# Low parts of the weights by an accumulating transfer in place of a subtraction on GpSimd

## The chip, the cores and the metric

The kernel runs on one core of one Trainium2 chip. The metric is the device time of one execution in microseconds; the whole input, weights included, lies in HBM at the start.

## What is computed

Two stacks of two layers each run over one sequence of 512 tokens of width 1024, in fp32. The first stack (`first_block`) has a convolution-and-attention mixer in layer 0, a gated linear recurrence in layer 1, and after each a squared-ReLU MLP of width 4096:

```python
for layer in range(DEPTH):
    h = rmsnorm(x, mix_norm[layer])
    y = mixer_ab(h, ...) if layer % 2 == 0 else mixer_c(h, ...)
    x = x + y
    x = x + sq_relu_mlp(rmsnorm(x, mlp_norm[layer]), w_up[layer], w_down[layer])
return rmsnorm(x, final_norm)
```

The second stack puts 16 meta tokens ahead (528 rows) and has, twice, a mixer of a gated delta rule and an indexed sparse attention, and a gated MLP of width 2816 with a short convolution:

```python
h = jnp.concatenate([meta, x], axis=1)
for l in range(DEPTH):
    n = rms_norm(h, norm_mix[l])
    h = h + hybrid_mixer(n, w_in[l], ...)
    n = rms_norm(h, norm_ffn[l])
    h = h + conv_gated_mlp(n, w_up[l], conv_ffn[l], w_down[l])
return h[:, N_META:]
```

## The kernel before, in words

Every product with a weight matrix is made with split operands. A value v is written as a high part (v rounded to fp32r, which TensorE reads in one pass) and a low part, v minus the high part, also fp32r. A product is three matmuls into the same PSUM bank: high weight by high value, high weight by low value, low weight by high value. In the code these are `for i, (w, v) in enumerate(((wh, hi), (wh, lo), (wl, hi)))`.

The weights come as 436 pieces of up to 512 KB (128 partitions x 1024 fp32). SyncE loads them in the order of use into `w_raw`, a ring of four slots (`load_piece`, L698). ScalarE copies a piece into `w_hi` (L1535), GpSimd subtracts, `w_lo` = `w_raw` - `w_hi`, in steps of 256 columns (L772). `w_hi` and `w_lo` are rings of eight half slots. The class `Order` plans what goes where. It holds 878 operations: a `whole` piece takes two half slots, the others one.

- In the mixers and at the start of each feed a piece is used whole (192 pieces).
- In the four feeds (mlp0, mlp1, and the gated MLPs layer0, layer1) the weights into the hidden layer are taken in pairs of pieces, and a pair is multiplied by seven half products in place of eight (a Strassen-like scheme): a11, s1, a12, s2, s4, s3, a22. Four of them need sums of weights that VectorE makes: s1, s2 and s4 into `weight_sum` (L2697, L2699, L2701), s3 in place in the raw slot of the pair's second piece (L2703). Between s3 and a22, and after a22, stand halves (`down`) of pieces of the second matrix. mlp0 and mlp1 have 14 pairs each with 4 such halves per pair (11 operations, 4 loads); layer0 and layer1 have 19 pairs each with 2 (9 operations, 3 loads).

The engines run in program order and wait on semaphores. What sets the order around the change:

- ScalarE (`split_one`) waits until the piece has landed, or the sum is made, and until the product that used the half slot before is done (`w_used`), then writes the high part and counts up `w_hi`. Between its splits it does the other work of the stage. In a feed it copies three products of each pair out of PSUM (`keep_product`, L1821, tile `kept_product`), which TensorE waits for before s2, s4 and s3 (L1035). Before each such copy it makes every split that is allowed by then (`split_before`).
- GpSimd does nothing but the low parts, in the same order, and counts up one semaphore `w_lo` per operation.
- TensorE waits for `w_lo` of an operation before its matmuls (L1035 for the half products, L1090 and L1094 for the down products, L800 for whole pieces).
- SyncE loads piece p + 4 when the last low part that reads the slot of piece p is made (`order.freed`). With three pieces to a gated pair, the second piece of the next pair needs the slot of this pair's first piece, which is free after the low part of s3.
- VectorE makes s1 of the next pair only when both its pieces have landed, and overwrites a `weight_sum` only when its old low part is made.
- In a gated feed VectorE takes a22 out of PSUM (L3181), multiplies (L3185, L3130) and makes s3 of the next pair (L2703).

```python
pool.wait_ge(w_hi, o + 1)
for a in range(0, n, 2 * P):
    z = min(a + 2 * P, n)
    i = pool.tensor_tensor(wl[:, slot, at + a:at + z], source[:, a:z],
                           wh[:, slot, at + a:at + z].bitcast(F32), ALU.subtract)
i.then_inc(w_lo, 1)
```

Of the kernel before, what the change touches and what calls it, by code (L numbers as in the profile page):

```python
# [220 lines left out]
class Order:  # L221
# [169 lines left out]
def build(nc, stream, xt, vec1, vec2, const1, const2, dist, lru_w, meta, saved_x, out):  # L391
# [172 lines left out]
    w_hi, w_lo, w_used = sem("w_hi_ready"), sem("w_lo_ready"), sem("w_product_done")  # L564
# [10 lines left out]
    mean_full, cent_ready, var_full, ln_root = sem("mean_full"), sem("centred_then_lru_rate"), sem("variance_full"), sem("ln_root_then_lru_rate_exp")  # L575
    ln_sq = sem("ln_square")
    ln_scaled, y_hi, y_ready = sem("ln_scaled"), sem("y_hi_ready"), sem("y_ready")
    bias_ready = sem("alibi_ready")
    vt_full, vt_copied, spread_copied = sem("v_turned"), sem("v_copied"), sem("head_scales_copied")
    s_full, s_shift, s_exp, heads_scaled = sem("scores_full"), sem("scores_shifted"), sem("scores_exp"), sem("head_scales_and_heads_ready")  # L580
    pt_full, pt_ready, o_full = sem("probs_turned"), sem("probs_t_ready"), sem("attn_out_full")
    xc_ready, ri_full, ri_sig, tanh_ready = sem("lru_conv_ready"), sem("head_scales_then_lru_gates_full"), sem("lru_sigmoid"), sem("lru_tanh")
    gelu_ready = sem("gelu_ready")
    xc_gated, x_final = sem("lru_input_gated"), sem("x_final")
    a_ready, m_ready, mult_ready, yc_ready = sem("lru_decay"), sem("lru_square"), sem("lru_mult"), sem("lru_out")
# [6 lines left out]
    vtok_full, vtok_ready = sem("v_tokens_full"), sem("v_tokens_ready")  # L592
# [4 lines left out]
    g_in, gcol_full = sem("decay_logs"), sem("decay_sums")  # L597
    norms_turned, first_tap = sem("norms_turned"), sem("first_tap_ready")
# [12 lines left out]
    ux_full, ux_ready, uy_full, uy_ready = sem("join_full"), sem("join_ready"), sem("last_join_full"), sem("last_join_ready")  # L611
    uw_full, uw_ready = sem("w_full"), sem("w_ready")
    uv_full, uv_ready, uso_full, us_ready, uo_done = sem("v_new_full"), sem("v_new_ready"), sem("step_full"), sem("state_ready"), sem("step_out_taken")
    oz_ready, o_hi, o_ready = sem("out_gated"), sem("out_hi_ready"), sem("out_lo_ready")
# [4 lines left out]
    meta_gained, both_sums, x_root = sem("meta_gained"), sem("both_sums_ready"), sem("x_root_ready")  # L619
    gate_sent = sem("gate_sent")  # L620
    gate_back = [sem(f"gate_back_{n}") for n in range(4)]

# [70 lines left out]
    def _(sp):  # L693
# [54 lines left out]
        for p in range(RAW_SLOTS, pieces):  # L748
            sp.wait_ge(w_lo, order.freed(p - RAW_SLOTS))
# [25 lines left out]

    @block.tensor
    def _(pe):
# [3 lines left out]
        def product(job, hi, lo, cols, wait=None):  # L781

            p = at["piece"]
            pe.wait_ge(w_lo, used(p + 1))
# [40 lines left out]
        def fill_wide(blocks):  # L825

            for _ in range(blocks):
                p, b = at["piece"], at["block"]
                if b == 0:
                    pe.wait_ge(w_lo, used(p + 1))  # L830
# [9 lines left out]
        def out_blocks(p, a, z, order, hi, lo):  # L840

            if a == 0:
                pe.wait_ge(w_lo, used(p + 1))
# [11 lines left out]
        def first_product():  # L855
# [3 lines left out]
            for b in range(KT + 4):  # L859
# [4 lines left out]
                if b == 4:  # L864
                    pe.wait_ge(w_lo, 1)
# [6 lines left out]
        def mixer0():  # L872
# [10 lines left out]
            def turn_v(pair):  # L883
# [7 lines left out]
                mm.then_inc(vt_full, 1)  # L891

            def scores(n):
# [3 lines left out]
                for hh in range(2):  # L897
                    half = slice(DH * hh, DH * hh + DH)
                    pe.matmul(aux[:, hh, 0:P * (i + 1)], qs[half, pair, P * i:P * i + P], ks[half, pair, 0:P * (i + 1)],
                              start=True, stop=True).then_inc(s_full, 1)  # L900
# [2682 lines left out]
```

## Time and profile before

| | |
|---|---|
| median of 3 runs | 2898.32 us (2896.45 to 2898.58) |
| the profiled execution | 2896.0 us |
| its span | 2894.2 us |
| granted TensorE clock, mean | 0.988 |
| TensorE matmul busy | 2737.9 us, 95% |
| VectorE busy | 2023.6 us, 70% |
| GpSimd busy | 1879.7 us, 65% |
| ScalarE busy | 1219.6 us, 42% |
| moved by DMA | 271.25 MB |

The span runs from the first to the last instruction of one profiled execution; the time of that execution is 1.8 us longer. Busy shares are means over stages with different limits, so the stages have to be looked at one by one. mlp0 lies at about 250 to 620 us, mlp1 at about 720 to 1090, the feed of layer0 at about 1640 to 2000, that of layer1 at about 2540 to 2890; the mixers lie between.

### The profile page before, as it was taken

What the parts mean: (1) busy time and instruction counts of PE and PEld (TensorE: products, weight loads), DVE (VectorE), ACT (ScalarE), POOL (GpSimd) and SP (SyncE); (2) the same over time, 40 slices, a digit from 0 to 9 for tenths busy, and PEclk for the clock granted to TensorE, in tenths of its full rate; (3) what the DMA queues carried; (4) which work ended last, traced back from release to release, by engine and by line L of the source; (5) the groups of instructions that cost most, each with busy time, mean ns of one, the idle gap of its engine ahead of it and who ended that gap; (6) DMA issues with size and microseconds to landing.
All of it is one profiled execution on the core that took longest, in us unless ns stands there. A gap on an engine that the chain in (4) does not pass through costs nothing.

```text
span 2894.2 us, 48195 instructions
## 1 busy us (share of the span) xinstructions
PE 2737.9 (95%) x18508; PEld 2470.3 (85%) x18508; DVE 2023.6 (70%) x3175; ACT 1219.6 (42%) x2145; POOL 1879.7 (65%) x2144
## 2 busy tenths in 40 slices
PE   9988999999899999999999889999999899988998
PEld 6767989877798988988899888999988799978887
DVE  8958666686666668897544777776797645767775
ACT  4454434455343444433343334445343353334442
POOL 6425998856599885532236589997542225489997
PEclk9999999999999999999999999999999999999999
DMA  5112332332233233323324122233322324122222
GB/s 185 59 34 75 96 110 94 111 102 75 72 100 105 95 117 111 110 66 96 105 83 133 54 81 93 91 100 108 100 78 88 89 87 142 60 86 84 88 90 93
DMA packets 122676, 271.25 MB, mean 94 GB/s; under 512 B 22864, under 2 KB 57040, under 8 KB 122192
## 3 DMA queue, kind: packets, MB, share of 16 engines
q1 hardware_dynamic: 73104, 245.98, 26.4%
q10 hardware_dynamic: 49344, 22.19, 2.8%
q8 instruction: 148, 2.42, 0.3%
q14 instruction: 80, 0.66, 0.1%
HBM read 249.52 MB, written 18.61 MB: 93 GB/s over the span
## 4 chain that ended last, share of the span: by engine, by line
PE 68%; DVE 22%; issue 5%; ACT 2%; POOL 1%; DMA 1%; ACTq 0%; SPq 0%; DVEq 0%
PE aux L1035 16%; PE acc L800 15%; PE acc L1090 13%; PE acc L1287 5%; PE acc L1094 3%; PE acc L849 3%; PE aux L1301 3%; DVE index_score L3227 2%; PE acc L1268 2%; PE aux L1268 2%; DVE best L3220 2%; DVE w_raw L2703 1%; DVE unit_b L3130 1%; POOL w_lo L772 1%; PE acc L833 1%
## 5 line engine op out<-in xcount | busy, mean ns | idle before, releaser
L772 POOL TENSOR_TENSOR w_lo<-w_raw,w_hi 128x256 fp32r<-128x256 f32 x1744 | 1478.5, 881 | 931.9 <-ACT w_hi L1535 928.1
L1535 ACT ACTIVATE w_hi<-w_raw 128x512 fp32r<-128x512 f32 (+2 forms) x680 | 487.2, 738 | 381.6 <-PE acc L800 143.7
L772 POOL TENSOR_TENSOR w_lo<-weight_sum,w_hi 128x256 fp32r<-128x256 f32 x396 | 407.2, 1054 | 61.2 <-ACT w_hi L1535 56.7
L1035 PE MATMUL aux<-token_sum_hi,w_hi 128*128 128x264 f32 (+1 forms) x1056 | 304.7, 289 | 77.6 <-ACT kept_product L1821 40.8
L800 PE MATMUL acc<-n_hi,w_hi 128*128 128x264 f32 (+1 forms) x1336 | 337.6, 317 | 8.8 <-DVE unit_a L3136 6.5
L800 PE MATMUL acc<-n_lo,w_hi 128*128 128x264 f32 (+1 forms) x1336 | 326.6, 309 | 0.0
L800 PE MATMUL acc<-n_hi,w_lo 128*128 128x264 f32 (+1 forms) x1336 | 326.0, 308 | 0.0
L1035 PE MATMUL aux<-token_sum_hi,w_lo 128*128 128x264 f32 (+1 forms) x1056 | 300.5, 285 | 0.0
L1035 PE MATMUL aux<-token_sum_lo,w_hi 128*128 128x264 f32 (+1 forms) x1056 | 300.3, 284 | 0.0
L1035 PEld LDWEIGHTS aux<-token_sum_hi,w_hi 128*128 128x128 f32 x1056 | 201.0, 190 | 90.8 <-issue 67.0
L1090 PE MATMUL acc<-hidden_hi,w_hi 128*128 128x512 f32 x688 | 271.9, 395 | 2.1 <-DVE hidden_lo L3109 2.1
L1090 PE MATMUL acc<-hidden_lo,w_hi 128*128 128x512 f32 x688 | 272.4, 396 | 0.0
L1090 PE MATMUL acc<-hidden_hi,w_lo 128*128 128x512 f32 x688 | 272.0, 395 | 0.0
L1535 ACT ACTIVATE w_hi<-weight_sum 128x512 fp32r<-128x512 f32 x198 | 124.8, 630 | 338.6 <-DVE weight_sum L2697 239.2
L2711 DVE TENSOR_TENSOR unit_a<-aux,kept_product 128x256 f32<-128x256 f32 (+1 forms) x160 | 68.3, 428 | 263.5 <-PE aux L1035 195.5
L800 PEld LDWEIGHTS acc<-n_hi,w_hi 128*128 128x128 f32 x1336 | 218.8, 189 | 37.8 <-issue 21.8
L800 PEld LDWEIGHTS acc<-n_lo,w_hi 128*128 128x128 f32 x1336 | 217.4, 189 | 14.3 <-issue 2.6
L1035 PE MATMUL aux<-n_hi,w_hi 128*128 128x264 f32 (+1 forms) x792 | 225.5, 285 | 4.2 <-POOL w_lo L772 4.0
L800 PEld LDWEIGHTS acc<-n_hi,w_lo 128*128 128x128 f32 x1336 | 217.4, 189 | 11.9
L1035 PE MATMUL aux<-n_lo,w_hi 128*128 128x264 f32 (+1 forms) x792 | 224.5, 283 | 0.0
L1035 PE MATMUL aux<-n_hi,w_lo 128*128 128x264 f32 (+1 forms) x792 | 224.5, 283 | 0.0
L2726 DVE TENSOR_TENSOR x<-x,acc 128x512 f32<-128x512 f32 (+1 forms) x224 | 153.2, 684 | 89.8 <-PE acc L1090 80.3
(525 smaller groups left out, 6364.3 us busy)
## 6 DMA issues: line engine op xcount, KB each, us to landing
w_raw<-in_stream SPq DMA_DIRECT2D x420, 512.0 KB, 3.6
unit_blocks<-unit_scratch ACTq DMA_DIRECT2D x26, 256.0 KB, 3.9
w_raw<-in_stream SPq DMA_DIRECT2D x16, 384.0 KB, 3.2
unit_scratch<-unit_staged ACTq DMA_DIRECT2D x20, 256.0 KB, 2.6
saved_x<-x SPq DMA_DIRECT2D x2, 2112.0 KB, 9.6
x<-saved_x SPq DMA_DIRECT2D x16, 264.0 KB, 2.7
saved_gates<-root ACTq DMA_DIRECT2D x12, 264.0 KB, 2.0
unit_scratch<-unit_staged ACTq DMA_DIRECT2D x1, 2560.0 KB, 15.1
```

The source lines that it names most:

```text
L772: i = pool.tensor_tensor(wl[:, slot, at + a:at + z], source[:, a:z], wh[:, slot, at + a:at + z].bitcast(F32), ALU.subtract)
L800: last = pe.matmul(o, w[:, slot_of(p), P * b:P * b + P], r, start=(b == 0 and i == 0), stop=(b == n - 1 and i == 2))
L849: mm = pe.matmul(acc[:, bank_of(p), :], w[:, slot_of(p), P * b:P * b + P], v[b], start=(n == 0 and i == 0), stop=(n == KT - 1 and i == 2))
L1035: mm = pe.matmul(aux[:, bank, 0:width], w[:, slot, at_ + P * b:at_ + P * b + P], v[:, b, :], start=(opens and b == 0 and i == 0), stop=(b ...
L1090: mm = pe.matmul(into, lhs, v[:, e % 2, b, ROW], start=(b == 0 and i == 0), stop=(b == n - 1 and i == 2))
L1094: mm = pe.matmul(banks[:, s, 0:HALF], lhs, v[:, e % 2, b, HALF * s:HALF * s + HALF], start=(b == 0 and i == 0), stop=(b == n - 1 and i == 2))
L1268: mm = pe.matmul(banks[:, 2 * g + s, 0:HALF], w[:, slot_of(p), P * b:P * b + P], v[:, b, HALF * s:HALF * s + HALF], start=(b == 4 * g and ...
L1287: mm = pe.matmul(acc[:, s, 0:HALF], w[:, slot_of(p), P * b:P * b + P], v[:, b, HALF * s:HALF * s + HALF], start=(b == 0 and i == 0), stop= ...
L1301: return pe.matmul(out, lhs, rhs, start=start, stop=stop)
L1535: act.activation(wh[:, slot, at_:at_ + n], weights_of(o), ACT.Copy).then_inc(w_hi, 1)
L2711: dve.tensor_tensor(into, aux[:, bank, 0:width], kept_product[:, kept, 0:width], ALU.add)\
L2726: dve.tensor_tensor(xm, xm, a, ALU.add).then_inc(taken, c.made(taken))
```

## The change

ScalarE now makes two activations per operation: first the negated value, rounded to fp32r, into `w_lo` (which is minus the high part), then the high part into `w_hi`. GpSimd no longer computes. For each operation it waits for the high part and issues one DMA that adds the fp32 values of `w_raw` (or `weight_sum`) onto `w_lo`, so that `w_lo` holds value minus high part when it lands. The one counter `w_lo` becomes eight semaphores, one per half slot of the ring, each raised by 16 per landing; everyone who waited for `w_lo` (TensorE, SyncE, VectorE) now waits for the landing of the operation it needs. `freed` returns the list of all operations that read a raw slot, and SyncE waits for each. To have eight semaphores free, several others with disjoint times of use are merged under one name.

```diff
@@ class Order
+        self.turn, turns = [], [0] * (2 * W_SLOTS)
...
+            turns[self.place[-1]] += 1
+            self.turn.append(turns[self.place[-1]])
...
     def freed(self, p):
 
-        found = [n + 1 for n, (kind, piece, _) in enumerate(self.ops) if piece == p or (piece == p - 1 and kind == "a22")]
-        paired = [n + 1 for n, (kind, piece, _) in enumerate(self.ops) if piece == p and kind == "s3"]
-        return paired[0] if paired else max(found)
+        return [n for n, (kind, piece, _) in enumerate(self.ops)
+                if (piece == p and kind in ("whole", "down", "a11", "a12", "s3")) or (piece == p - 1 and kind in ("a22", "s3"))]
@@ build
-    w_hi, w_lo, w_used = sem("w_hi_ready"), sem("w_lo_ready"), sem("w_product_done")
+    w_hi, w_used = sem("w_hi_ready"), sem("w_product_done")
+    w_lo = [sem(f"w_lo_landed_{n}") for n in range(2 * W_SLOTS)]
...
+    def low_landed(o):
+
+        return w_lo[order.place[o]], 16 * order.turn[o]
@@ SyncE
         for p in range(RAW_SLOTS, pieces):
-            sp.wait_ge(w_lo, order.freed(p - RAW_SLOTS))
+            for o in order.freed(p - RAW_SLOTS):
+                sp.wait_ge(*low_landed(o))
             load_piece(p)
@@ GpSimd
             pool.wait_ge(w_hi, o + 1)
-            for a in range(0, n, 2 * P):
-                z = min(a + 2 * P, n)
-                i = pool.tensor_tensor(wl[:, slot, at + a:at + z], source[:, a:z],
-                                       wh[:, slot, at + a:at + z].bitcast(F32), ALU.subtract)
-            i.then_inc(w_lo, 1)
+            pool.dma_start(wl[:, slot, at:at + n], source, accum_op=ALU.add).then_inc(low_landed(o)[0], 16)
@@ TensorE, at each wait for a low part
-                pe.wait_ge(w_lo, o + 1)
+                pe.wait_ge(*low_landed(o))
@@ ScalarE
             n = width_of(o)
+            act.activation(wl[:, slot, at_:at_ + n], weights_of(o), ACT.Copy, scale=-1.0)
             act.activation(wh[:, slot, at_:at_ + n], weights_of(o), ACT.Copy).then_inc(w_hi, 1)
@@ VectorE, weight_sum_of
-            if name != "s3" and at["split"][n]:
-                dve.wait_ge(w_lo, at["split"][n])
-            at["split"][n] = order.index[name, p, u] + 1
+            if name != "s3" and at["split"][n] is not None:
+                dve.wait_ge(*low_landed(at["split"][n]))
+            at["split"][n] = order.index[name, p, u]
```

On ScalarE, in the feed of layer0, around the first `kept_product` of a pair: the high parts of s3 and of the two down halves, the copy of a11's product, the high part of a22, and the copy of s1's product. Before:

```order
L1535 ACTIVATE w_hi<-weight_sum 128x512 x2
L1535 ACTIVATE w_hi<-w_raw 128x512 x3
L1821 ACTIVATE kept_product<-aux 128x264
L1535 ACTIVATE w_hi<-w_raw 128x512
L1821 ACTIVATE kept_product<-aux 128x264
```

The same place in the changed program:

```order
L1538 ACTIVATE w_lo<-w_raw 128x512
L1539 ACTIVATE w_hi<-w_raw 128x512
L1538 ACTIVATE w_lo<-w_raw 128x512
L1539 ACTIVATE w_hi<-w_raw 128x512
L1538 ACTIVATE w_lo<-w_raw 128x512
L1539 ACTIVATE w_hi<-w_raw 128x512
L1825 ACTIVATE kept_product<-aux 128x264
L1538 ACTIVATE w_lo<-w_raw 128x512
L1539 ACTIVATE w_hi<-w_raw 128x512
L1825 ACTIVATE kept_product<-aux 128x264
```

Six activations stand ahead of the first copy where three stood, and two ahead of the second where one stood.

On GpSimd, over one pair of the same feed (s2 and s4 from `weight_sum`; then s3, two down halves, a22 and the next a11 from `w_raw`; the next s1; the next a12). Before:

```order
L772 TENSOR_TENSOR w_lo<-weight_sum,w_hi 128x256 x4
L772 TENSOR_TENSOR w_lo<-w_raw,w_hi 128x256 x10
L772 TENSOR_TENSOR w_lo<-weight_sum,w_hi 128x256 x2
L772 TENSOR_TENSOR w_lo<-w_raw,w_hi 128x256 x2
```

Now:

```order
L777 DMA w_lo<-weight_sum 128x512 x2
L777 DMA w_lo<-w_raw 128x512 x5
L777 DMA w_lo<-weight_sum 128x512
L777 DMA w_lo<-w_raw 128x512
```

The order is the same; two subtractions of 256 columns have become one transfer of 512.

## Rows read from the trace of the kernel before

**Rows 1.** The page, part 1: busy us, share of the span and count by engine
```profile
PE 2737.9 (95%) x18508; PEld 2470.3 (85%) x18508; DVE 2023.6 (70%) x3175; ACT 1219.6 (42%) x2145; POOL 1879.7 (65%) x2144
```

**Rows 2.** Windows: stretch, its length, busy us (x count) by engine, clock, DMA share, GB/s
```profile
core 0: us, PE busy (x) PEld busy (x) DVE busy (x) ACT busy (x) POOL busy (x), PEclk, DMA share, GB/s
...
300.00:400.00 100.00, 100.00 (x620) 89.34 (x619) 64.79 (x87) 40.56 (x78) 93.98 (x108) 1.00 0.32 101
...
1200.00:1300.00 100.00, 97.28 (x781) 90.44 (x780) 95.22 (x228) 40.94 (x59) 42.50 (x53) 1.00 0.25 75
...
1800.00:1900.00 100.00, 93.83 (x763) 92.73 (x762) 73.58 (x96) 41.65 (x81) 99.14 (x105) 1.00 0.29 93
```

**Rows 3.** Waits of TensorE over the span: us in total, times, longest us
```profile
PE aux L1035 <- ACT kept_product L1821: 40.8, 33, 1.8
PE aux L1035 <- POOL w_lo L772: 24.8, 7, 8.6
PE aux L1035 <- DVE root L2711: 14.9, 12, 2.6
```

**Rows 4.** The page, part 5: GpSimd's two groups
```profile
L772 POOL TENSOR_TENSOR w_lo<-w_raw,w_hi 128x256 fp32r<-128x256 f32 x1744 | 1478.5, 881 | 931.9 <-ACT w_hi L1535 928.1
...
L772 POOL TENSOR_TENSOR w_lo<-weight_sum,w_hi 128x256 fp32r<-128x256 f32 x396 | 407.2, 1054 | 61.2 <-ACT w_hi L1535 56.7
```

**Rows 5.** Timeline of ScalarE, feed of layer0: start us, us for all, instruction, [idle before]
```profile
1785.33 1.67 ACT L1535 ACTIVATE w_hi<-w_raw 128x512 fp32r<-128x512 f32 x3 [3.26 <-DVE w_raw L2703]
1786.91 0.37 ACT L1821 ACTIVATE kept_product<-aux 128x264 f32<-128x264 f32 x1
...
1804.21 0.37 ACT L1821 ACTIVATE kept_product<-aux 128x264 f32<-128x264 f32 x1
```

**Rows 6.** Timeline of TensorE there: the first matmul of s2
```profile
1787.43 0.36 PE L1035 MATMUL aux<-token_sum_hi,w_hi 128*128 128x264 f32 x1 [1.03 <-ACT kept_product L1821]
```

**Rows 7.** Timeline of VectorE there
```profile
1780.72 0.68 DVE L2701 TENSOR_TENSOR weight_sum<-w_raw,weight_sum 128x512 f32<-128x512 f32 x1
...
1782.05 0.43 DVE L3181 TENSOR_TENSOR root<-aux,norm_scale 128x264 f32<-128x264 f32 x1
1782.40 0.59 DVE L3185 TENSOR_TENSOR root<-root,norm_scale 128x264 f32<-128x264 f32 x1
1783.12 1.03 DVE L3130 TENSOR_TENSOR unit_b<-squares,root 128x528 f32<-128x528 f32 x1
1784.08 1.22 DVE L2703 TENSOR_TENSOR w_raw<-w_raw 128x512 f32<-128x512 f32 x1
...
1791.90 1.22 DVE L2697 TENSOR_TENSOR weight_sum<-w_raw 128x512 f32<-128x512 f32 x1
...
1794.04 2.29 DVE L3122 SCALAR_TENSOR_TENSOR unit_b<-unit_a,vec,unit_b 128x528 f32<-128x528 f32 x2
```

**Rows 8.** The page, part 3: the queue of the weight loads, share of 16 engines
```profile
q1 hardware_dynamic: 73104, 245.98, 26.4%
```

**Rows 9.** DMA issues: count, KB each, us to landing; and one load's issue, feed of layer0
```profile
w_raw<-in_stream SPq DMA_DIRECT2D x9, 512.0 KB, 3.7
...
unit_blocks<-unit_scratch ACTq DMA_DIRECT2D x26, 256.0 KB, 3.9
...
unit_scratch<-unit_staged ACTq DMA_DIRECT2D x20, 256.0 KB, 2.6
...
1787.48 0.33 SPq L698 DMA_DIRECT2D w_raw<-in_stream  x1
```

**Rows 10.** DMA from 1780 to 1830 us in 40 slices: busy tenths, GB/s
```profile
DMA  0000004730369300000057105792000000670048
GB/s 0 0 0 0 0 0 36 262 134 0 26 256 419 144 0 0 0 0 0 7 85 282 66 0 52 269 419 98 0 0 13 0 0 0 88 305 26 0 69 331
```

**Rows 11.** Timeline of ScalarE in mlp0, the same copy in two pairs
```profile
397.75 0.39 ACT L1821 ACTIVATE kept_product<-aux 128x256 f32<-128x256 f32 x1
...
418.75 0.39 ACT L1821 ACTIVATE kept_product<-aux 128x256 f32<-128x256 f32 x1
```

**Rows 12.** Timeline of GpSimd, feed of layer0: s3, two down halves, a22, next a11
```profile
1786.05 8.56 POOL L772 TENSOR_TENSOR w_lo<-w_raw,w_hi 128x256 fp32r<-128x256 f32 x10
```

More of the change, by code:

```diff
@@ L783, in product @@
             p = at["piece"]
-            pe.wait_ge(w_lo, used(p + 1))
+            pe.wait_ge(*low_landed(used(p)))
             one, paired = cols == SEQ, job >= starts.get("layer0", pieces)
@@ L829, in fill_wide @@
                 if b == 0:
-                    pe.wait_ge(w_lo, used(p + 1))
+                    pe.wait_ge(*low_landed(used(p)))
                     pe.wait_ge(taken, evicted(p) - 1)
@@ L842, in out_blocks @@
             if a == 0:
-                pe.wait_ge(w_lo, used(p + 1))
+                pe.wait_ge(*low_landed(used(p)))
                 pe.wait_ge(taken, evicted(p) - (1 if shares(p) else 3))
@@ L864, in first_product @@
                 if b == 4:
-                    pe.wait_ge(w_lo, 1)
+                    pe.wait_ge(*low_landed(0))
                 if b >= 4:
@@ L890, in turn_v @@
                     mm = pe.transpose(acc[:, 1, P * a:P * a + P], vs[:, pair, P * a:P * a + P], ident)
-                mm.then_inc(vt_full, 1)
+                mm.then_inc(vtok_full, 1)
             def scores(n):
@@ L1124, in narrow_product @@
             p = at["piece"]
-            pe.wait_ge(w_lo, used(p + 1))
+            pe.wait_ge(*low_landed(used(p)))
             if half == 0:
@@ L1259, in branch @@
             if g:
-                pe.wait_ge(w_lo, used(p + 1))
+                pe.wait_ge(*low_landed(used(p)))
                 pe.wait_ge(taken, evicted(p) - (1 if m else 0))
@@ L1280, in fill @@
             if at["block"] == 0:
-                pe.wait_ge(w_lo, used(p + 1))
+                pe.wait_ge(*low_landed(used(p)))
                 pe.wait_ge(taken, evicted(p))
@@ L1617, in norm_twice @@
             act.wait_ge(ss_full, c.next(ss_full))
-            act.wait_ge(both_sums, 1)
+            act.wait_ge(both_sums, c.next(both_sums))
             act.activation(rt[:, :], ssq[:, :], ACT.Sqrt, scale=1.0 / D).then_inc(root_ready, c.made(root_ready))
@@ L1660, in copy_v @@
             def copy_v(pair):
-                act.wait_ge(vt_full, pair + 1)
+                act.wait_ge(vtok_full, c.next(vtok_full))
                 act.activation(vt[:, :, P * pair:P * pair + P], acc[:, 1, :].rearrange("p (a d) -> p a d", a=4),
@@ L1711, in mixer0 @@
                         act.wait_ge(cent_ready, c.next(cent_ready))
-                        act.activation(zpad[:, i, 0:SEQ], cv[:, i, :], ACT.Square).then_inc(ln_sq, c.made(ln_sq))
+                        act.activation(zpad[:, i, 0:SEQ], cv[:, i, :], ACT.Square).then_inc(vtok_ready, c.made(vtok_ready))
                 if n == 13:
@@ L1721, in mixer0 @@
                     for i in range(4):
-                        act.wait_ge(ln_scaled, c.next(ln_scaled))
+                        act.wait_ge(both_sums, c.next(both_sums))
                         act.activation(zpad[:, i, 0:SEQ], cv[:, i, :], ACT.Silu, scale=vec("ab_ln_g", i),
@@ L1745, in gates_of @@
                 act.activation(tb[:, h, :], rb[:, h, :], ACT.Tanh, scale=c8[:, 2, h:h + 1])\
-                    .then_inc(tanh_ready, c.made(tanh_ready))
+                    .then_inc(first_tap, c.made(first_tap))
             def decay(h):
@@ L1761, in high_of @@
             def high_of(h):
-                act.wait_ge(yc_ready, h + 1)
+                act.wait_ge(oz_ready, c.next(oz_ready))
                 act.activation(y1_hi[h], xc[:, h, :], ACT.Copy).then_inc(y_hi, c.made(y_hi))
@@ L2286, in _ @@
         c = Counts()
-        at = {"piece": 0, "squared": False, "low": 0, "split": [0, 0, 0, 0]}
+        at = {"piece": 0, "squared": False, "low": 0, "split": [None] * 4}
         def step(i):
@@ L2443, in shift @@
                     dve.wait_ge(pt_full, n - 1)
-                dve.wait_ge(s_full, 2 * n + hh + 1)
+                dve.wait_ge(ux_full, c.next(ux_full))
                 dve.tensor_tensor_reduce(sm[:, b, 0:w], aux[:, hh, 0:w], bias[:, hh, SEQ - w:SEQ], 1.0, 3e38,
@@ L2481, in mixer0 @@
                 if n == 12:
-                    dve.wait_ge(mean_full, 1)
+                    dve.wait_ge(gcol_full, c.next(gcol_full))
                     for i in range(4):
@@ L2490, in mixer0 @@
                         dve.tensor_tensor(cv[:, i, :], cv[:, i, :], ub[:, 0, 0:SEQ], ALU.mult)\
-                            .then_inc(ln_scaled, c.made(ln_scaled))
+                            .then_inc(both_sums, c.made(both_sums))
                 if n == 15:
@@ L2572, in square_of_mult @@
             def square_of_mult(h):
-                dve.wait_ge(tanh_ready, h + 1)
+                dve.wait_ge(first_tap, c.next(first_tap))
                 dve.wait_ge(a_ready, 2 * h + 1)
@@ L2589, in mixed @@
                 dve.wait_ge(*scanned[h])
-                dve.tensor_tensor(xc[:, h, :], tb[:, h, :], gb[:, h, :], ALU.mult).then_inc(yc_ready, c.made(yc_ready))
+                dve.tensor_tensor(xc[:, h, :], tb[:, h, :], gb[:, h, :], ALU.mult).then_inc(oz_ready, c.made(oz_ready))
             def low(h):
```

31 lines of the change are left out of this document (15 added, 16 removed).

## The prediction

> **What bounds the kernel now.** I read the page first, then the windows, the waits of TensorE, and last one period of the timeline. TensorE is busy 95% of the span [rows 1], so at most some 156 us (2894.2 minus 2737.9) are to be had. The windows [rows 2] show three kinds of stretch. In mlp0 (300 to 400 us) TensorE is never idle, and GpSimd is busy 94%. In the mixers (1200 to 1300 us) VectorE is the busy one, at 95%, and TensorE loses under 3%. In the gated feed of layer0 (1800 to 1900 us) GpSimd is busy 99% and TensorE loses 6%. The waits of TensorE [rows 3] name 40.8 us for `kept_product` (ScalarE), 24.8 us for `w_lo` (GpSimd) and 14.9 us for a VectorE sum. So GpSimd's subtractions, 1478.5 + 407.2 us [rows 4], are nearly hidden: what they cost directly is the 24.8 us.
>
> They cost something indirectly. In the gated feed a pair takes 17.30 us: `kept_product` begins at 1786.91 and again at 1804.21 [rows 5]. In each period TensorE stands still 1.03 us before s2, for ScalarE's `kept_product` [rows 6]. That copy is late because ScalarE first has to write three high parts, which begin when VectorE has made the sum s3, at 1785.33 [rows 5]. VectorE starts on the work before s3 when a22 has left TensorE (L3181 at 1782.05) and ends s3 at 1785.30 [rows 7]. Its s3 sum takes 1.22 us, the same shape in L2701 0.68 us [rows 7]. GpSimd's own operations of one shape differ as well, 881 and 1054 ns on the mean [rows 4]. I read both as the two engines holding each other up, now one waiting, now the other.
>
> **The change part by part.** One profiled execution of 2896.0 us (span 2894.2) is what I add to; the median of the runs is 2898.32, within 0.1%, so I make no correction. About 0.2% (6 us) is what a measurement can tell from nothing.
>
> (1) *Removed: 2140 subtractions on GpSimd.* The direct waits of 24.8 us [rows 3] go, if the transfers come in time: -25. VectorE speeds up. From the s1 sum to the s3 sum it gains 0.54 on s1 and s3 each (1.22 to 0.68), some 0.9 on the two L3122 (2.29 for two, against 0.68 for one of that size) and 0.35 on L3130 [rows 7]. But s3 also waits for a22 from TensorE. Counted from there the gain is 0.54 + 0.35 and some 0.2 on L3185, 1.1 us.
>
> (2) *Added: 878 negated copies on ScalarE.* Three activations take 1.67 us [rows 5], so one of 512 columns adds 0.53 us of pitch. Ahead of `kept_product` stand three of them: +1.58 us. Against 1.1 us won on VectorE the stall before s2 grows by 0.45 us, from 1.03 to 1.5 us. With 19 pairs in each of two layers that is 38 x 0.45 = 17 us if nothing else were later. In mlp0 and mlp1 (28 pairs, 21.00 us each [rows 11]) `kept_product` is copied as soon as its product is done and needed three products later, so the extra ScalarE time is covered. In the mixers ScalarE is busy 41% [rows 2]; a 1024-column copy more per piece sits between steps of softmax and the like, while VectorE there gets a little faster. I set the two against each other at 0, with bounds of -30 and +30 us.
>
> (3) *Added: 878 accumulating transfers.* The trace of before has none, and no transfer issued by GpSimd. One for a half piece carries 256 KB. The nearest rows are the weight loads: 512 KB hold the 16 DMA engines 1.6 us on the mean (26.4% of 2894.2 us for 245.98 MB [rows 8]); where two came back to back they ran at up to 419 GB/s and took some 1.3 us each [rows 10]. An addition has to read both source and destination, so I price 256 KB of it as 512 KB of load: 1.3 to 1.6 us. The lower bound is one pass, 0.65 us; the upper one is a transfer that nothing overlaps, 2.6 us, the whole time to landing of a 256 KB store [rows 9]. I take two passes, as the operation must read twice. By itself stands this: the Trainium skill (Collectives: The Full Stack, "The bandwidth ceiling: the fold count and why AG ≠ RS ≠ AR") explains a reduction at half a copy's rate by its two source reads on one read ring; no run here shows it yet.
>
> *Occupancy.* A gated pair has 9 half pieces and 3 loads, 12 units: 15.6 us at 1.3, 19.6 us at 1.63, against the period of 17.30. An mlp pair has 11 half pieces and 4 loads, 15 units: 19.5 to 24.5 us against 21.00. A whole piece in a mixer needs 3 units, 3.9 to 4.9 us, and TensorE has some 6.1 us for it (48 matmuls at 781 per 100 us [rows 2]): covered.
>
> *Latency.* The tightest loop in the gated feed runs through the four raw slots. s3 is made (ends 1785.30), ScalarE writes its high part, GpSimd its low part (from 1786.05 [rows 12]), SyncE may load into the slot (issue 1787.48), the load lands 3.7 us later [rows 9], and with it VectorE starts the next s1 sum at 1791.90 [rows 7]. That is 6.6 us, 0.7 of it slack. After the change: ScalarE 1.15, the transfer some 4.7 (3.9 us for a 256 KB gather from the rows [rows 9], and 0.8 for the second read), the load 3.7 or, among the new traffic, 4.5: 10.4 us, 3.8 more. VectorE makes up 2.0 us of it (0.54 on s1, 0.9 on L3122, 0.54 on s3); the rest, 1.8 us, falls on the period. Occupancy (up to +2.3) and latency (+1.8) do not add, since the queue is a part of the latency. I take +2.3 us: 38 x 2.3 = 87 us, which contains the 0.45 us of (2). For the mlp pairs the loop has over 8 us to spare (s1 is needed long after), so occupancy alone counts: 0 to 3.5 us per pair; I take 2.0, since the transfers come in bursts of seven: 28 x 2.0 = 56 us.
>
> (4) *Waits.* SyncE waits on one to three semaphores per load in place of one; it sits in that wait 2.5 ms anyway. What stands behind it is only the next load. GpSimd never waits for a landing. Merged semaphores change no order. Nothing here costs time: 0.
>
> Sum: 2896 - 25 + 87 + 56 = 3014 us. What is late next is the low part of s3: TensorE wants it 24 matmuls after s2 begins, 2.9 us at 763 matmuls in 93.83 us [rows 2].
>
> **The rivals.**
> A. *The transfers keep up and the kernel gets faster.* For this speaks that DMA is busy only a third of the time (0.29 in the gated window [rows 2]) and that GpSimd was at 99%. Then the wait for `w_lo` (24.8 us) and the one for VectorE (14.9 us) go and the longer queue on ScalarE costs 17: 2896 - 40 + 17 = 2873 us; if the wait for `kept_product` went too, 2816. It decides at a transfer that lands within 3.7 us of the high part (6.6 of the loop + 2.0 won on VectorE - 1.15 - 3.7 for the load). By the Trainium skill (DMA: Bandwidth & Descriptors, "Anatomy of one DMA") a GpSimd transfer takes about 2.0 us plus its bytes at 436 GB/s, an estimate of 2.6 us for 256 KB, which would give this rival; no row of this trace shows such a transfer. Against it stand the two reads and the loads beside them. Chance 0.25.
>
> B. *The transfers are worked off one after another*, by GpSimd's issuing or by additions that don't overlap, at 2.6 us each (upper bound above). Then an mlp pair takes 11 x 2.6 = 28.6 us (+7.6), a gated pair 9 x 2.6 = 23.4 us (+6.1): 2896 - 25 + 28 x 7.6 + 38 x 6.1 = 3316 us. Chance 0.23. For it: the page shows nothing on either rate.
>
> C. *Gains and losses cancel* near 2896: chance 0.07. That the change doesn't do what it says can be left out: each half piece is now one DMA on GpSimd and two activations on ScalarE.
>
> **How the numbers follow.** The forecast, two passes and a loop longer by some 2 us, has 0.45; its own range is 2940 to 3090 us (ends of the occupancy). Faster by over 0.2%: A, 0.25. Within 0.2%: C, 0.07. Slower: forecast and B, 0.68. The range for 8 in 10 goes from 2860 (A, but for the case that all of ScalarE's wait goes) to 3330 (B, but for transfers yet slower).
>
> **What would show it.** Right: DMA share of 0.75 to 0.95 in both feeds; TensorE waiting there for DMA of `w_lo`; s1 and s3 sums at 0.7 us; a gated period near 19.6 and an mlp period near 23 us. Landing of an accumulating transfer 4 to 6 us after its issue. Wrong: periods of 17.7 and 21.0 us with landings of 3 us (rival A), or a GpSimd queue that is issuing without a break or landings over 8 us with periods over 23 and 28 us (rival B).

## The result, and the profile after

The changed kernel takes 3023.85 us (median of 4 runs, 3019.2 to 3028.59) against 2898.45 us before: ratio 1.0434, 95% interval 1.0416 to 1.0452. The forecast was 3014 us. The profiled execution took 3019.2 us, its span is 3017.4 us.

The page of the changed kernel, parts 1 and 3, answers to [rows 1] and [rows 8]:

```profile
PE 2784.5 (92%) x18508; PEld 2495.8 (83%) x18508; DVE 1672.1 (55%) x3175; ACT 1728.9 (57%) x3023; POOL 757.0 (25%) x882
...
q0 software_dynamic: 126432, 278.45, 52.6%
q1 hardware_dynamic: 73104, 245.98, 25.5%
```

VectorE needs 351 us less for the same 3175 instructions, ScalarE 509 us more, GpSimd 1123 us less. The new queue q0, the one of the accumulating transfers, holds the 16 DMA engines 52.6% of the span: 1587 us for 278.45 MB, 1.49 us for 256 KB. I call such a time the occupancy of a transfer. Before, nothing of that was there.

Where the time went shows best from feed to feed. The instructions that make the s1 sums, 14 in an mlp feed and 19 in a gated one, give each feed a first and a last time. Before, the source line L2697, in the four feeds (ns min/median/max, first to last start in us):

```profile
L2697 DVE TENSOR_TENSOR weight_sum<-w_raw x14: 674/984/1227, 258.0 to 532.0; 128x512 f32<-128x512 f32 x14
L2697 DVE TENSOR_TENSOR weight_sum<-w_raw x14: 684/1078/1221, 763.9 to 1037.8; 128x512 f32<-128x512 f32 x14
L2697 DVE TENSOR_TENSOR weight_sum<-w_raw x19: 684/1217/1226, 1627.2 to 1947.6; 128x512 f32<-128x512 f32 x19
L2697 DVE TENSOR_TENSOR weight_sum<-w_raw x19: 683/1224/1229, 2521.2 to 2841.8; 128x512 f32<-128x512 f32 x19
```

The same line in the changed kernel (L2701):

```profile
L2701 DVE TENSOR_TENSOR weight_sum<-w_raw x14: 681/692/695, 261.3 to 576.8; 128x512 f32<-128x512 f32 x14
L2701 DVE TENSOR_TENSOR weight_sum<-w_raw x14: 680/692/694, 801.3 to 1115.3; 128x512 f32<-128x512 f32 x14
L2701 DVE TENSOR_TENSOR weight_sum<-w_raw x19: 684/692/694, 1692.9 to 2046.6; 128x512 f32<-128x512 f32 x19
L2701 DVE TENSOR_TENSOR weight_sum<-w_raw x19: 684/692/694, 2618.2 to 2965.8; 128x512 f32<-128x512 f32 x19
```

Every s1 sum now takes 0.69 us; in the gated feeds most took 1.22, in the mlp feeds about 1.0 on the median. From these times (all stretches between them, the start and the tail added as "the rest"; a pair's period is the length by 13 or 18):

| span us | mlp0 | mlp1 | layer0 feed | layer1 feed | the rest | in all |
|---|---|---|---|---|---|---|
| before | 274.0 | 273.9 | 320.4 | 320.6 | 1705.3 | 2894.2 |
| changed | 315.5 | 314.0 | 353.7 | 347.6 | 1686.6 | 3017.4 |
| difference | +41.5 | +40.1 | +33.3 | +27.0 | -18.7 | +123.2 |
| pair's period, before | 21.1 | 21.1 | 17.8 | 17.8 | | |
| pair's period, changed | 24.3 | 24.2 | 19.7 | 19.3 | | |

The windows show the load of each engine in the feeds. They answer to [rows 2]; columns as there:

```profile
400.00:500.00 100.00, 90.30 (x544) 78.83 (x543) 41.25 (x75) 54.52 (x108) 37.94 (x44) 1.00 0.98 207
...
1900.00:2000.00 100.00, 88.66 (x681) 86.00 (x680) 49.17 (x86) 60.45 (x119) 39.08 (x47) 0.97 0.97 203
```

In these stretches no engine is above 91%, and the DMA share is 0.98 and 0.97; in the feed windows of [rows 2] it was 0.32 and 0.29. The waits of TensorE in the changed kernel, against [rows 3]:

```profile
PE aux L1038 <- ACT kept_product L1825: 69.2, 74, 2.0
PE aux L1038 <- DMA w_lo<-weight_sum: 57.5, 34, 7.0
PE aux L1038 <- DVE root L2715: 34.5, 18, 5.7
```

And the landings, from the page's part 6 (count, KB each, median us from issue to landing):

```profile
w_raw<-in_stream SPq DMA_DIRECT2D x420, 512.0 KB, 5.1
w_lo<-w_raw POOLq DMA_DIRECT2D x456, 256.0 KB, 5.9
w_lo<-w_raw POOLq DMA_DIRECT2D x192, 512.0 KB, 5.7
w_lo<-weight_sum POOLq DMA_DIRECT2D x198, 256.0 KB, 4.3
```

A load of 512 KB that landed in 3.6 us takes 5.1 us. One turn of the loop through the raw slots can be read in mlp0. From the timelines of VectorE, ScalarE and GpSimd there (start us, us, instruction, [idle before]): the s1 sum of one pair,

```profile
410.11 0.69 DVE L2701 TENSOR_TENSOR weight_sum<-w_raw 128x512 f32<-128x512 f32 x1 [8.33 <-issue]
...
414.86 0.69 DVE L2707 TENSOR_TENSOR w_raw<-w_raw 128x512 f32<-128x512 f32 x1
...
433.86 0.69 DVE L2701 TENSOR_TENSOR weight_sum<-w_raw 128x512 f32<-128x512 f32 x1 [7.14 <-issue]
```

then ScalarE's two activations for s3 and, after those for two down halves, the copy that TensorE waits for,

```profile
416.72 0.62 ACT L1538 ACTIVATE w_lo<-w_raw 128x512 fp32r<-128x512 f32 x1
417.24 0.62 ACT L1539 ACTIVATE w_hi<-w_raw 128x512 fp32r<-128x512 f32 x1
...
419.84 0.36 ACT L1825 ACTIVATE kept_product<-aux 128x256 f32<-128x256 f32 x1
```

and GpSimd's issue for a22, whose landing frees the slot for the load that the next s1 sum needs:

```profile
421.54 0.86 POOL L777 DMA_DIRECT2D w_lo<-w_raw  x1 [0.45 <-ACT w_hi L1539]
```

From 410.11 to 421.54 are 11.4 us of VectorE and ScalarE, from there to 433.86 are 12.3 us: the issue, a landing and a load. VectorE stands still 7.1 us before the sum. The turn takes 23.75 us.

In the gated feeds the same loop shows as waits. From 1700 to 1900 us, in the feed of layer0:

```profile
DVE weight_sum L2701 <- DMA w_raw<-in_stream: 29.7, 9, 7.5
```

```profile
PE aux L1038 <- DVE root L2715: 16.5, 7, 5.7
PE aux L1038 <- DMA w_lo<-weight_sum: 7.4, 5, 2.8
PE aux L1038 <- ACT kept_product L1825: 7.0, 8, 2.0
```

VectorE works in program order and stands before the s1 sum until the load has landed. `root`, which TensorE waits for, comes behind that sum: at 1759.69 us VectorE starts the sum after a wait of 7.48 us, and at 1762.31 `root`. So more than half of TensorE's waiting there is for VectorE, and VectorE waits for a load.

### The profile page after: what moved, and what is told of

Its sections match the earlier page's. It is cut to its first block, busy times and chain, and to the rows that moved or that the text cites. A ratio compares the mean times of both kernels' runs of the same rounds, so it can differ in the third digit from the quotient of the medians.

```text
span 3017.4 us, 48049 instructions
## 1 busy us (share of the span) xinstructions
PE 2784.5 (92%) x18508; PEld 2495.8 (83%) x18508; DVE 1672.1 (55%) x3175; ACT 1728.9 (57%) x3023; POOL 757.0 (25%) x882
## 3 DMA queue, kind: packets, MB, share of 16 engines
q0 software_dynamic: 126432, 278.45, 52.6%
## 4 chain that ended last, share of the span: by engine, by line
PE 45%; DMA 20%; DVE 15%; issue 10%; ACT 9%; ACTq 1%; POOL 0%; DVEq 0%; SPq 0%
PE acc L803 19%; DMA w_raw<-in_stream 9%; DMA w_lo<-w_raw 9%; PE acc L1093 5%; PE aux L1038 4%; ACT w_hi L1539 4%; PE acc L1290 3%; PE acc L852 2%; ACT w_lo L1538 2%; PE aux L1304 2%; PE acc L1097 2%; PE acc L836 2%; DVE weight_sum L2701 1%; DVE index_score L3231 1%; DVE best L3224 1%
## 5 line engine op out<-in xcount | busy, mean ns | idle before, releaser
L777 POOL DMA_DIRECT2D w_lo<-w_raw x680 | 587.3, 870 | 1772.4 <-ACT w_hi L1539 1707.4
L1538 ACT ACTIVATE w_lo<-w_raw 128x512 fp32r<-128x512 f32 (+2 forms) x680 | 500.8, 737 | 381.9 <-DMA w_raw<-in_stream 167.4
L1539 ACT ACTIVATE w_hi<-w_raw 128x512 fp32r<-128x512 f32 (+2 forms) x680 | 498.1, 733 | 0.0
L1038 PE MATMUL aux<-token_sum_hi,w_hi 128*128 128x264 f32 (+1 forms) x1056 | 320.4, 303 | 160.8 <-ACT kept_product L1825 68.6
L1038 PE MATMUL aux<-token_sum_hi,w_lo 128*128 128x264 f32 (+1 forms) x1056 | 306.8, 291 | 0.0
L1538 ACT ACTIVATE w_lo<-weight_sum 128x512 fp32r<-128x512 f32 x198 | 124.1, 627 | 303.4 <-DVE weight_sum L2701 287.2
L777 POOL DMA_DIRECT2D w_lo<-weight_sum x198 | 170.8, 871 | 465.4 <-ACT w_hi L1539 458.1
```

Of the source, the lines that this page charges most:

```text
L777: pool.dma_start(wl[:, slot, at:at + n], source, accum_op=ALU.add).then_inc(low_landed(o)[0], 16)
L1038: mm = pe.matmul(aux[:, bank, 0:width], w[:, slot, at_ + P * b:at_ + P * b + P], v[:, b, :], start=(opens and b == 0 and i == 0), stop=(b ...
L1538: act.activation(wl[:, slot, at_:at_ + n], weights_of(o), ACT.Copy, scale=-1.0)
L1539: act.activation(wh[:, slot, at_:at_ + n], weights_of(o), ACT.Copy).then_inc(w_hi, 1)
```

## The experiments

The expectations speak of three theories of the slowdown. O: the DMA engines are full in the feeds. L: the transfer's time to landing makes the loop through the raw slots longer. S: ScalarE's second activation costs the time.

**A plain copy in place of the addition.** All transfers stay, with their bytes, but nothing is added and the destination is not read; the low part is then the whole weight, so the result is wrong.

```diff
-            pool.dma_start(wl[:, slot, at:at + n], source, accum_op=ALU.add).then_inc(low_landed(o)[0], 16)
+            pool.dma_start(wl[:, slot, at:at + n], source).then_inc(low_landed(o)[0], 16)
```

> The changed kernel with a plain copy in place of the accumulating transfer: as many transfers, as many bytes landed, but the destination is not read (the low part is then the whole weight, so a part of the computation is changed). Theory O (the 16 DMA engines are full in the feeds, because an addition reads twice): 256 KB should hold the engines some 0.75 us in place of 1.49, an mlp pair then needs 15 us and a gated pair 12 us of DMA, both under TensorE's own time, and the kernel falls to 2880 to 2920 us with a DMA share near 0.7 in the feeds. Theory L (the fixed latency of a transfer in the loop through the raw slots): landings get shorter by 1 us at most, and the time stays above 2980 us. Theory S (ScalarE's second copy): no change, 3024 us.

Measured: 2880.44 us, ratio to before 0.993 (0.9914 to 0.9946). The page, part 3:

```profile
q0 software_dynamic: 126432, 278.45, 29.7%
```

29.7% of 2880.4 us for the same bytes are 0.81 us for 256 KB, against 1.49 us: the addition costs 1.85 times a copy on the engines. The median landing of a 256 KB transfer from `w_raw` falls from 5.9 to 3.3 us. The feeds take 279.7, 275.2, 325.5 and 321.3 us, within 6 us of before each, although ScalarE still makes both activations. So adding in place of copying, the read of the destination with it, is worth 143 us in the change; without it the rest of the change is a gain of 18 us. Theory S falls as the explanation of the whole. That landings shorten by 1 us at most, as theory L had it, is wrong: 2.6 us. The run changes one more thing: GpSimd's issue of a transfer falls from 0.87 to 0.53 us. The next run keeps 0.87 us and takes the same time, so that is not the cause.

**Half the columns.** Each transfer adds the first half of its columns only; the other half of the low part stays minus the high part, so the result is wrong.

```diff
-            pool.dma_start(wl[:, slot, at:at + n], source, accum_op=ALU.add).then_inc(low_landed(o)[0], 16)
+            pool.dma_start(wl[:, slot, at:at + n // 2], source[:, 0:n // 2], accum_op=ALU.add).then_inc(low_landed(o)[0], 16)
```

> The changed kernel, but each accumulating transfer adds only the first half of its columns (the rest of the low part stays minus the high part, a changed computation): as many transfers, still accumulating, half the bytes, rows of 1 KB. Theory O: 0.75 us per operation, 2880 to 2930 us. Theory L: fixed part of the latency unchanged, above 2970 us. If an addition costs by the row and not by the byte, occupancy stays near 1.5 us per operation and the time at 3024 us.

Measured: 2881.32 us, ratio 0.9939 (0.992 to 0.9958).

```profile
q0 software_dynamic: 126432, 139.25, 31.4%
```

31.4% of 2881.5 us for 139.25 MB are 0.85 us for what was a 256 KB operation: 0.64 us less for half the bytes, so by this estimate some 1.28 of 1.49 us go by the byte and 0.2 by the transfer or its 128 rows, which this run does not tell apart. The loss goes with the bytes that are added, not with the number of transfers or a fixed latency. Landings got shorter too (5.9 to 3.6 us from `w_raw`), so this run alone does not part full engines from a longer loop.

**ScalarE's second activation alone**, in the kernel before; GpSimd overwrites what it wrote.

```diff
+            act.activation(wl[:, slot, at_:at_ + n], weights_of(o), ACT.Copy, scale=-1.0)
             act.activation(wh[:, slot, at_:at_ + n], weights_of(o), ACT.Copy).then_inc(w_hi, 1)
```

> The kernel before with ScalarE's additional negated copy into the low part, which GpSimd then overwrites with its subtraction as before: ScalarE's part of the change alone. Theory O with the prediction's step (2): the copy of a product ahead of s2 comes 1.58 us later in each of 38 gated pairs, which VectorE does not make up here as GpSimd still slows it: 2896 + 60 = 2956 us, nothing in the mlp feeds. Theory S: ScalarE explains the change, 3000 to 3030 us. If ScalarE is covered: 2896 to 2905 us.

Measured: 2980.77 us, ratio 1.0278 (1.0262 to 1.0293), 25 us more than the sum said. By the s1 sums the gated feeds take 351.5 and 351.7 us, +62 together, where the +1.58 us of step (2) in each of 38 pairs gave 60; the mlp feeds +8, the rest +14. The wait of TensorE named in that step grew from 40.8 to

```profile
PE aux L1035 <- ACT kept_product L1822: 93.4, 40, 3.0
```

A single wait is now up to 3.0 us, 1.2 more than the longest before. So ScalarE's copy is not covered in the gated feeds as long as VectorE is slow. How well 62 fits 60 says less than it seems, because the granted clock fell as well. A window of the feed of layer0:

```profile
1800.00:1900.00 100.00, 88.27 (x668) 87.17 (x667) 61.03 (x87) 59.32 (x115) 75.00 (x91) 0.93 0.24 80
```

Over the two gated feeds it reads 0.95 and 0.94, where it was 0.99 and 0.98. That is 39 us of full-speed work lost against 10 us, so some 29 of the 62 us may be the clock, by these rounded figures. No run separates the two. The plain copy run has the same activations and VectorE relieved, reads 0.99 in both feeds, and is 6 us above before in the two gated feeds together.

**No negated copy**, in the changed kernel; the transfers add onto whatever the slot held, so the result is wrong.

```diff
-            act.activation(wl[:, slot, at_:at_ + n], weights_of(o), ACT.Copy, scale=-1.0)
+            if o < 8:
+                act.activation(wl[:, slot, at_:at_ + n], weights_of(o), ACT.Copy, scale=-1.0)
```

> The changed kernel without the negated copy (but for the first eight operations), so the transfers add onto what the slot held; the low parts are wrong in value. Transfers and latencies are those of the change, ScalarE's load is that of before. Theory O: the feeds stay full, 3000 to 3020 us. Theory S: falls to about 2900 us. Theory L: each loop is 0.5 us shorter, 66 pairs by 0.5 us, about 2990 us.

Measured: 2978.54 us, ratio 1.0273 (1.0254 to 1.0292): 45 us less than the change, below theory O's range and 12 us below what L gave. The two mlp feeds take 299.1 and 297.0 us, 33 less than with the copy, a period of 22.9 us; the gated feeds take 360.3 and 347.5, not less than with it; the stretches outside the feeds give 17 us. In mlp0 the DMA share stays full:

```profile
300.00:400.00 100.00, 96.44 (x600) 85.52 (x600) 42.28 (x77) 34.61 (x68) 42.37 (x49) 1.00 1.06 221
```

So in the mlp feeds some of ScalarE's extra activations lie in the loop shown above, and without them the period falls to about what the occupancy gives (11 x 1.49 and 4 loads of 1.64, 23.0 us; 23.5 at the 1.54 us that a half piece alone takes, as seen below). This window moves 221 GB/s at a share of 1.06, the change moved 211 in the same window at 1.01: a share near 1 is not yet the most that the engines do, and a sum of occupancies is good to a few per cent only. In the gated feeds the wait for `kept_product` nearly goes (3.4 us over the span, 69.2 in the change), but the wait for `root`, behind VectorE's s1 sum, grows from 34.5 to

```profile
PE aux L1038 <- DVE root L2716: 84.5, 34, 8.1
```

and the feeds gain nothing: there ScalarE's extra activations are not what sets the period.

**Which transfer is shortened: s3 and a22, or s2 and s4.** Both runs shorten two transfers of every pair to half their columns and so save the same occupancy. The first pair of operations frees raw slots, the second does not. What is left out makes the result wrong. The first run's edit; the second has `('s2', 's4')` in its place:

```diff
+            if kind in ('s3', 'a22'):
+                n = n // 2
-            pool.dma_start(wl[:, slot, at:at + n], source, accum_op=ALU.add).then_inc(low_landed(o)[0], 16)
+            pool.dma_start(wl[:, slot, at:at + n], source[:, 0:n], accum_op=ALU.add).then_inc(low_landed(o)[0], 16)
```

> The changed kernel in which the transfers of s3 and a22 alone add only half their columns (their low parts are then partly wrong). These two free the raw slots for the next loads. Theory O (occupancy): two operations of a pair get 0.64 us shorter each (1.49 to 0.85, by the run with half columns), so each of the 66 pairs gains up to 1.3 us: mlp periods 24.2 to 22.9, gated periods 19.5 to 18.3, 2940 to 2960 us. Theory L (the loop s3, transfer, load, s1): at least as much, and in the gated feed more than the next run shows.

> The same with s2 and s4 in place of s3 and a22: the same bytes and rows saved, but these two read weight sums and free no raw slot. Theory O: like the run before, within 10 us of it. Theory L: the gated period stays near 19.5, so some 45 us slower than the run before; the mlp feeds gain alike in both.

Measured: 2945.33 us (ratio 1.0167, 1.0151 to 1.0183) for s3 and a22, 2994.11 us (1.0328, 1.0305 to 1.0351) for s2 and s4. The s1 sums of the layer1 feed in the first and in the second run:

```profile
L2703 DVE TENSOR_TENSOR weight_sum<-w_raw x19: 681/692/693, 2565.3 to 2897.3; 128x512 f32<-128x512 f32 x19
```

```profile
L2703 DVE TENSOR_TENSOR weight_sum<-w_raw x19: 684/692/694, 2588.9 to 2930.8; 128x512 f32<-128x512 f32 x19
```

The four feeds together gain 67 us with s3 and a22 and 31 us with s2 and s4. TensorE's waits for the low parts of weight sums, 57.5 us in the change, are in the first and in the second run

```profile
PE aux L1040 <- DMA w_lo<-weight_sum: 33.9, 20, 7.0
```

```profile
PE aux L1040 <- DMA w_lo<-weight_sum: 60.6, 32, 7.0
```

Two of the three low parts that this wait can be for are those that the second run makes shorter, and it does not fall there; it falls when s3 and a22 get shorter, whose landings free the slots for the loads of the next s1 sum. Neither theory had it alone: L came near with the 49 us between the runs (it said 45), but not with the mlp feeds alike, and O wanted the runs within 10 us. Both runs gain, so full engines are a part; where a transfer stands decides by a factor of two, so the loop through the raw slots is a part too. And it is so in the mlp feeds as well (30 against 14 us), where the prediction had given the loop over 8 us to spare.

**Hybrids that compute the whole result.** One kernel with a choice by operation: ScalarE writes the negated copy and GpSimd issues a transfer where `by_transfer(o)` holds; everywhere else GpSimd subtracts and counts up one semaphore as before. Two first choices:

```diff
+            if by_transfer(o):
                 pool.dma_start(wl[:, slot, at:at + n], source, accum_op=ALU.add).then_inc(low_landed(o)[0], 16)
+                continue
+            for a in range(0, n, 2 * P):
+                z = min(a + 2 * P, n)
+                i = pool.tensor_tensor(wl[:, slot, at + a:at + z], source[:, a:z],
+                                       wh[:, slot, at + a:at + z].bitcast(F32), ALU.subtract)
+            i.then_inc(low_landed(o)[0], 1)
...
+        return kind == "whole"                         # the first
+        return gated and kind in ("s2", "s4")          # the second
```

> A hybrid that computes the whole result: accumulating transfers for whole pieces alone (192 of 878 operations, the mixers and the starts of the feeds), GpSimd's subtraction and ScalarE's single copy for all operations of the pairs and their down halves. If the change gains outside the feeds by relieving VectorE (18.7 us in the profile of the change, 26.6 in the plain copy run) and loses only inside, this is faster than before by 10 to 27 us: 2870 to 2888. If the gain there comes only with less work of GpSimd in the feeds: 2895 to 2900.

> A hybrid that computes the whole result: accumulating transfers only for s2 and s4 of the 38 gated pairs (76 operations). ScalarE idles at that place, and GpSimd is then not subtracting while VectorE makes the terms up to s3, so the stall of 1.03 us before s2 should go: 38 x 1.0 = 39 us, 2858 to 2870 us. If landings take over 5 us TensorE waits for them instead: 2895 us or more.

Measured: 2878.84 us (ratio 0.9942, 0.993 to 0.9955) with whole pieces, 2857.09 us (0.986, 0.9844 to 0.9875) with s2 and s4 of the gated pairs. Queue q0 holds the engines 4.1% of 2854.4 us for the 76 transfers of the second, 1.54 us each: that is a half piece alone, the 1.49 us above are a mean with the whole pieces. In the second the gated feeds take 303.2 and 298.1 us, 40 less together. The timeline of VectorE and ScalarE there, against [rows 7] and [rows 5]:

```profile
1808.07 0.43 DVE L3209 TENSOR_TENSOR root<-aux,norm_scale 128x264 f32<-128x264 f32 x1
1808.42 0.42 DVE L3213 TENSOR_TENSOR root<-root,norm_scale 128x264 f32<-128x264 f32 x1
1808.97 0.71 DVE L3158 TENSOR_TENSOR unit_b<-squares,root 128x528 f32<-128x528 f32 x1
1809.60 0.68 DVE L2731 TENSOR_TENSOR w_raw<-w_raw 128x512 f32<-128x512 f32 x1
```

```profile
1810.32 1.67 ACT L1563 ACTIVATE w_hi<-w_raw 128x512 fp32r<-128x512 f32 x3 [1.71 <-DVE w_raw L2731]
1811.90 0.37 ACT L1849 ACTIVATE kept_product<-aux 128x264 f32<-128x264 f32 x1
```

From the start of a22's way out of PSUM (L3209) to the end of s3 VectorE needs 2.21 us, where it needed 3.25: 1.04 us less, as much as TensorE's stall of 1.03 us before s2. In this turn 0.68 us of waiting are left; over the span the wait for `kept_product`, 40.8 us before, is

```profile
PE aux L1061 <- ACT kept_product L1849: 4.9, 10, 0.7
```

In a window of the feed TensorE is busy again:

```profile
1800.00:1900.00 100.00, 99.28 (x808) 98.16 (x807) 73.11 (x104) 49.81 (x96) 90.73 (x99) 1.00 0.47 127
```

**Both, and a control.** The choices of the two hybrids in one; and, as a control, as many transfers in the same pairs but for a11 and a22.

```diff
+        return kind == "whole" or (gated and kind in ("s2", "s4"))
+        return gated and kind in ("a11", "a22")        # the control
```

> Both hybrids in one, whole result: accumulating transfers for the 192 whole pieces and for s2 and s4 of the 38 gated pairs (268 of 878 operations). If the two gains are of separate stretches they add: 2898 - 19 - 41 = 2838 us. If the whole pieces' transfers only repeat a gain that the other has: 2855.

> The control for the hybrid with s2 and s4: as many transfers in the same pairs (76), but for a11 and a22, so whole result and GpSimd relieved by the same number of subtractions. If it is GpSimd's load of 99% that matters: 2855 to 2870 us as there. If it is that VectorE must not be slowed between a22's product and the s3 sum (GpSimd works on s2 and s4 then): the period stays at 17.3 or grows by up to 0.5 us for ScalarE's copy of a22 ahead of the second kept_product, 2895 to 2915 us.

Measured: both 2838.81 us, ratio 0.9798 (0.978 to 0.9815), the best of all kernels here; the control 2883.29 us, ratio 0.9951 (0.9936 to 0.9967). The gains add, within 1 us of the sum expected. The control lies between its two forecasts, faster than I expected: its gated feeds take 314.3 and 307.6 us, 19 less together. VectorE is quicker at s1 (0.69 us) there, but L3213, which took 0.42 us in the hybrid above, is still slow while GpSimd works on s2 and s4:

```profile
1813.25 0.86 DVE L3213 TENSOR_TENSOR root<-root,norm_scale 128x264 f32<-128x264 f32 x1
...
1817.68 0.36 PE L1061 MATMUL aux<-token_sum_hi,w_hi 128*128 128x264 f32 x1 [0.45 <-ACT kept_product L1849]
```

From L3209 (1812.90) to the end of s3 (1815.56) VectorE needs 2.66 us, 0.59 less than before, and the stall before s2 is 0.45 us, 0.58 less. It is the first `kept_product` that ends this stall, and the control's extra activation, for a22, comes behind that copy, so it is not ScalarE that makes the control slower. In three kernels (before, control, hybrid) this stretch of VectorE takes 3.25, 2.66 and 2.21 us, and TensorE waits for `kept_product` 40.8, 24.1 and 4.9 us over the span. So 76 operations fewer for GpSimd at another place of the pair give 19 us in these feeds, at the right place 40.

## Why the prediction was right, and where it was not

The time was met within 10 us. The mechanism was right in its main parts, but that the sum came so near is in part luck. By stretches of the profile, 25 us of gain did not come, the mlp feeds lost 26 us more than forecast, the gated feeds 27 less, and the rest gained 19 that were put at nothing: 5 us in all.

- *Mechanism.* Engines full or nearly so in both feeds, a loop made longer, VectorE relieved: shown. The price of an addition was put at 1.3 to 1.6 us for 256 KB and measured 1.49; the plain copy run shows that adding makes it. That it is the second read and not the arithmetic is not shown by any run. By the Trainium skill (Collectives: The Full Stack, "The bandwidth ceiling: the fold count and why AG ≠ RS ≠ AR") a reduction runs at about half a copy's rate because it reads two sources; this case agrees in size, 1.49 against 0.81 us, 1.85 times. Of the signs that I gave, the sums at 0.7 us, the landings (5.9 and 4.3 us) and the gated period came as said; the DMA share came out above its range, 0.98 and 0.97 for at most 0.95.
- *Step (3), mlp feeds.* Predicted +56 us (period 23.0), measured +81.6 (24.2). The step that failed is "the loop has over 8 us to spare, so occupancy alone counts". With the landing of a22 and the next load, some 12 us together, the loop fills the whole period (23.75 us in the turn shown), and ScalarE's second activations, held covered there in step (2), lie in the same loop: without them the period is 22.9.
- *Step (3), gated feeds.* Predicted 19.6 us a pair, measured 19.7 and 19.3; but +87 us was too much, measured +60.3. I had subtracted the 17.30 us of a quiet stretch, where the mean of the feed before is 17.8, so the term was mis-sized in its base. That its end was met is partly luck as well: 19.6 us came from occupancy alone at 1.63 us for 256 KB. At the 1.54 us measured for a half piece the sum is 9 x 1.54 + 3 x 1.64 = 18.8 us, and the rest of the period is waiting in the loop and a lower clock.
- *Step (1), the wait for GpSimd, -25 us.* It did not go. Those waits stand at the starts of the feeds (8.6 us in each mlp feed), before products with weight sums; by stretches they are 8.6, 8.6, 4.0 and 3.5 us before and 9.4, 7.0, 2.8 and 2.9 us after, then for the transfer. The plain copy still waits up to 6.0 us at a time in mlp0. In the change, in mlp0, ScalarE starts on the first sum only at 266.12 us, 4 us after VectorE has made it, because `hidden_hi` comes first and waits for VectorE; the transfer is issued at 267.55 and TensorE goes on at 270.86. So half of this wait of 7.0 us passes before the transfer is issued; I had put the wait to GpSimd by its name.
- *Step (2), ScalarE.* The arithmetic of +1.58 us per gated pair with VectorE unrelieved gave 60 us, the run 62, a part of it the clock. Against a relieved VectorE I gave +0.45 us; the plain copy run has +0.3 and +0.04.
- *The mixers*, set at 0 between -30 and +30, gave -18.7 us with start and tail: there VectorE's relief outweighs ScalarE's load. ScalarE's activations alone cost 14 us in these stretches (the run on the kernel before), and the change without them gains 35.
- *What is late next* was to be the low part of s3. It is not: s3 is read from `w_raw`, and TensorE waits for such low parts in the half products 5.2 us in all, for those of weight sums 57.5 us, for `kept_product` 69.2 us and for `root` 34.5 us.

Rival A (the transfers keep up, 2873 us) did not come about. The plain copy, which does keep up, gives 2880, but by other terms: its four feeds are 13 us longer than before, where A had 23 us of gain, and the stretches outside them 27 us shorter, which A put at 0. The estimate by the Trainium skill (DMA: Bandwidth & Descriptors, "Anatomy of one DMA"), 2.6 us for 256 KB, was not met by the additions, 5.9 and 4.3 us in the changed kernel; of the plain copies those from `weight_sum` met it with 2.6 us, those from `w_raw` took 3.3. Rival B (one after another, 2.6 us each) falls by the occupancy of 1.49 us and by GpSimd's issue, 0.87 us each.

What stays open: how much of the 60 us in the gated feeds is the loop and how much the full engines. A run with a fifth raw slot would tell it; there is none. Part may be the clock, below.

## What to carry to other kernels

A transfer that adds is priced at nearly two copies (1.85 here), and the engines' time is summed over the busiest stretch, not over the span: 30% of DMA use on the mean was room for the copy but not for the addition in the feeds. Before an idle stretch of a loop is called slack, every stage that the change lengthens is put into it at once. And moving work off an engine pays where another engine waits on the contention: 76 of the 878 transfers brought 41 us, all of them cost 125.

## What the runs showed of the hardware that I had not expected

The additions run at 1.85 times a copy's occupancy, and what does not go by the byte is small: an estimated 0.2 of 1.49 us in a transfer of 128 rows. GpSimd's issue of such a transfer holds its queue 0.87 us (0.53 us for a plain copy), less than the 1.7 to 2.1 us of the two subtractions that it replaces, and VectorE's sums beside it stay at 0.69 us (the 19 of the layer0 feed lie between 684 and 694 ns), so issuing did not slow these sums as subtracting did.

The granted clock fell more often. The mean is 0.981 against 0.988; the four feeds read 0.98, 0.99, 0.97 and 0.96, before 0.99, 0.98, 0.99 and 0.98. Two windows of 10 us, one behind the other, in the layer0 feed of the changed kernel:

```profile
1750.00:1760.00 10.00, 6.57 (x52) 6.17 (x51) 1.45 (x3) 2.09 (x5) 2.61 (x3) 0.96 1.01 219
1760.00:1770.00 10.00, 7.12 (x46) 7.15 (x47) 7.88 (x14) 6.65 (x13) 3.88 (x5) 0.69 0.73 158
```

TensorE was busy 6.6 us of ten, and in the next ten the clock was at its lower level, 1.2 GHz in place of 2.4, for a part. A mean of 0.97 and 0.96 over the two gated feeds is 354 x 0.03 + 348 x 0.04 = 25 us of full-speed work lost, against 321 x 0.01 + 321 x 0.02 = 10 us before. By these rounded figures that is some 15 of the 60 us, and in the windows shown it came after waiting. No run separates it.
